# Moving matmul operands by 8 to 48 bytes off multiples of 64 in SBUF, in a two-layer trunk on one core

## The reference

```python
def short_conv_mixer(h, w_in, conv_w, w_out):
    bcx = h @ w_in                       # 1024 -> 3 x 1024
    u = c_gate * xp
    u_conv = causal_depthwise_conv3(u)
    return (b_gate * u_conv) @ w_out

def swiglu(h, w_gate, w_up, w_down):
    return (jax.nn.silu(h @ w_gate) * (h @ w_up)) @ w_down

for i in range(2):
    mixer = mla_mixer if i == 0 else short_conv_mixer
    h = h + mixer(rms_norm(h))
    h = h + swiglu(rms_norm(h))
return rms_norm(h)
```

## Time and profile before

| | |
|---|---|
| median of 3 runs | 1104.34 us (1103.94 to 1104.73) |
| the profiled execution's own time | 1105.14 us |
| its span in the trace | 1103.4 us, so 1.7 us lie around it |
| TensorE busy | 98% |
| LDWEIGHTS busy | 87% |
| VectorE busy | 67% |
| ScalarE busy | 41% |
| DMA | 26.7% of 16 engines, 96 GB/s |
| TensorE on the chain that ended last | 93% |

### The profile page before, as it was taken

The page is one execution under the profiler, slowest core; times in us unless marked ns, Lnnn a source line. Parts: engine busy times, 40 slices in busy tenths (PEclk is TensorE's granted clock), DMA queues, the critical chain, the costliest instruction groups (busy, mean ns, idle before and its releaser), DMA issues.

```text
span 1103.4 us, 16219 instructions
## 1 busy us (share of the span) xinstructions
PE 1081.8 (98%) x6208; PEld 956.0 (87%) x6208; DVE 734.9 (67%) x1013; ACT 454.2 (41%) x621; POOL 40.7 (4%) x22
## 2 busy tenths in 40 slices
PE   9999999998999999999999999999989999999997
PEld 7888888887999999888888888888879999988886
DVE  6667766698788887733447446677878888773332
ACT  5667763333445545521231212224345455452221
POOL 0232230000000000000000000000000000000000
PEclk9999999999899999999999999999989999999999
DMA  7211211322232232232222332223222332222211
GB/s 272 102 67 48 76 50 65 115 87 95 87 114 89 101 114 105 77 105 105 105 76 77 115 115 85 107 76 115 77 83 108 114 114 79 112 105 105 72 61 76
DMA packets 16964, 106.17 MB, mean 96 GB/s; under 512 B 1889, under 2 KB 2145, under 8 KB 6433
## 3 DMA queue, kind: packets, MB, share of 16 engines
q1 hardware_dynamic: 16848, 105.43, 26.7%
q0 software_dynamic: 80, 0.26, 0.1%
HBM read 103.59 MB, written 2.10 MB: 96 GB/s over the span
## 4 chain that ended last, share of the span: by engine, by line
PE 93%; DVE 4%; ACT 1%; DMA 1%; issue 0%; SPq 0%; DVEq 0%; ACTq 0%
PE bank L453 31%; PE bank L454 30%; PE bank L455 30%; PE bank L607 1%; PE bank L593 1%; DMA head<-head_in 1%; DVE w_lo L1450 0%; DVE x_lo L1481 0%; ACT w_hi L1007 0%; DVE rstd L1178 0%; DVE s_lo L1452 0%; DVE work L1183 0%; ACT w_hi L793 0%; DVE work L1442 0%; DVE work L1440 0%
## 5 line engine op out<-in xcount | busy, mean ns | idle before, releaser
L793 ACT ACTIVATE w_hi<-raw 128x2048 fp32r<-128x2048 f32 (+1 forms) x66 | 118.6, 1797 | 277.9 <-PE bank L455 277.8
L1146 DVE TENSOR_TENSOR w_lo<-raw,w_hi 128x2048 fp32r<-128x2048 f32 (+2 forms) x58 | 126.8, 2186 | 104.1 <-ACT w_hi L793 104.1
L453 PE MATMUL bank<-x_hi,w_hi 128*128 128x256 f32 x512 | 146.3, 286 | 10.5 <-DVE inner L1508 10.5
L454 PE MATMUL bank<-x_lo,w_hi 128*128 128x256 f32 x512 | 146.0, 285 | 0.0
L455 PE MATMUL bank<-x_hi,w_lo 128*128 128x256 f32 x512 | 145.9, 285 | 0.0
L453 PE MATMUL bank<-inner_hi,w_hi 128*128 128x512 f32 x352 | 137.0, 389 | 0.0
L454 PE MATMUL bank<-inner_lo,w_hi 128*128 128x512 f32 x352 | 137.0, 389 | 0.0
L455 PE MATMUL bank<-inner_hi,w_lo 128*128 128x512 f32 x352 | 136.9, 389 | 0.0
L453 PE MATMUL bank<-a_hi,w_hi 128*128 128x512 f32 x296 | 117.2, 396 | 1.9 <-DVE a_lo L1236 1.5
L455 PE MATMUL bank<-a_hi,w_lo 128*128 128x512 f32 x296 | 115.4, 390 | 0.0
L454 PE MATMUL bank<-a_lo,w_hi 128*128 128x512 f32 x296 | 115.3, 390 | 0.0
(11 more groups left out here) (207 smaller groups left out, 2111.3 us busy)
## 6 DMA issues: line engine op xcount, KB each, us to landing
raw<-weights_in SPq DMA_DIRECT2D x82, 1024.0 KB, 4.8
raw<-weights_in SPq DMA_DIRECT2D x12, 768.0 KB, 4.2
raw<-weights_in SPq DMA_DIRECT2D x6, 512.0 KB, 3.7
work<-x SPq DMA_DIRECT2D x4, 512.0 KB, 6.1
head<-head_in SPq DMA_DIRECT2D x3, 512.0 KB, 8.5
out<-head SPq DMA_DIRECT2D x3, 512.0 KB, 3.3
out<-head SPq DMA_DIRECT2D x2, 256.0 KB, 4.0
head<-head_in SPq DMA_DIRECT2D x1, 293.5 KB, 3.5
```

Of the source, the lines that this page charges most:

```text
L453: pe.matmul(o, lhs[0], rhs[0], start=start, stop=False, skip_group_check=True)
L454: pe.matmul(o, lhs[0], rhs[1], start=False, stop=False, skip_group_check=True)
L793: act.activation(w_hi[s][:, 0:n], raw[s][:, 0:n], ACT.Copy).then_inc(hi_split[s], 1)
L1146: v.tensor_tensor(w_lo[s][:, 0:n], raw[s][:, 0:n], w_hi[s][:, 0:n], ALU.subtract).then_inc(w_split[s], 1)
```

## The change

Only places in SBUF change. Each tensor that TensorE reads gets a start that is moved by some bytes; `placed` learns to place at any multiple of 4 bytes (it allocates from the multiple of 32 below and slices). Four 8-column tensors of the softmax move into the arena, since the row is nearly full.

```diff
+LINE = 64
+SLOT_OFF = (4, 2)
-SUMS_AT = [0, 6 * TILE_BYTES]
-FORMS_AT = 12 * TILE_BYTES
-INNER_AT = 40 * TILE_BYTES
+SUMS_AT = [16, 6 * TILE_BYTES + 48]
+FORMS_AT = 12 * TILE_BYTES + LINE + 0
+INNER_AT = 40 * TILE_BYTES + 2 * LINE
 INNER_HI_AT = 0
-FFN_IN_AT = INNER_AT + 2 * PLAIN_ROUNDS * TILE_BYTES
-MIXER_IN_AT = KF * TILE_BYTES
-CONV_AT = HEAD_OUT_AT = (0, KD * TILE_BYTES)
+FFN_IN_AT = INNER_AT + 2 * PLAIN_ROUNDS * TILE_BYTES + 0
+MIXER_IN_AT = KF * TILE_BYTES + LINE + 32
+HEAD_OUT_AT = (0, KD * TILE_BYTES)
+CONV_AT = (16, KD * TILE_BYTES + 16)
+NUMBERS_AT = 18 * TILE_BYTES
-MID_AT = [(38 + i * MID_TILES) * TILE_BYTES for i in range(2)]
+MID_AT = [(38 + i * MID_TILES) * TILE_BYTES + 2 * LINE for i in range(2)]
...
-            return nc.alloc_sbuf_tensor_at(name, [P, cols], dt, offset=arena_at + at)
+            off = at % 32
+            return nc.alloc_sbuf_tensor_at(name, [P, cols + off // 4], dt, offset=arena_at + at - off)[:, off // 4:off // 4 + cols]
...
-        w_hi = [sb(f"w_hi{s}", SLOT, F32R) for s in range(2)]
-        w_lo = [sb(f"w_lo{s}", SLOT, F32R) for s in range(2)]
+        w_hi, w_lo = ([sb(f"{n}{s}", SLOT + LINE // 4, F32R)[:, off:off + SLOT] for s, off in enumerate(SLOT_OFF)] for n in ("w_hi", "w_lo"))
...
-        row_max, exp_bias, row_sum, row_inv = (sb(n, 8) for n in ("row_max", "exp_bias", "row_sum", "row_inv"))
+        row_max, exp_bias, row_sum, row_inv = (placed(n, NUMBERS_AT + 32 * i, 8, F32)
```

More of the change, by code:

```diff
@@ L89 @@
 TILE_BYTES = SEQ * 4
-SUMS_AT = [0, 6 * TILE_BYTES]
-FORMS_AT = 12 * TILE_BYTES
-INNER_AT = 40 * TILE_BYTES
-INNER_HI_AT = 0
-FFN_IN_AT = INNER_AT + 2 * PLAIN_ROUNDS * TILE_BYTES
-MIXER_IN_AT = KF * TILE_BYTES
-CONV_AT = HEAD_OUT_AT = (0, KD * TILE_BYTES)
+LINE = 64
[3 more added lines that the diff above has]
+INNER_AT = 40 * TILE_BYTES + 2 * LINE
+INNER_HI_AT = 0
+FFN_IN_AT = INNER_AT + 2 * PLAIN_ROUNDS * TILE_BYTES + 0
[3 more added lines that the diff above has]
+NUMBERS_AT = 18 * TILE_BYTES
 SIN_AT, SQ_AT = 16 * TILE_BYTES, 17 * TILE_BYTES
-MID_AT = [(38 + i * MID_TILES) * TILE_BYTES for i in range(2)]
-ARENA = (38 + 2 * MID_TILES) * TILE_BYTES
+MID_AT = [(38 + i * MID_TILES) * TILE_BYTES + 2 * LINE for i in range(2)]
+ARENA = (38 + 2 * MID_TILES) * TILE_BYTES + 2 * LINE
 PI_BELOW = 3.1415925
@@ L205, in build @@
         ident, ones = sb("ident", P), sb("ones", P)
-        row_max, exp_bias, row_sum, row_inv = (sb(n, 8) for n in ("row_max", "exp_bias", "row_sum", "row_inv"))
+        row_max, exp_bias, row_sum, row_inv = (placed(n, NUMBERS_AT + 32 * i, 8, F32)
+                                               for i, n in enumerate(("row_max", "exp_bias", "row_sum", "row_inv")))
         numbers = sb("numbers", 9 * TOK + 2)
```

## The result

The changed kernel takes 1111.59 us (median of 3 runs, 1110.77 to 1112.41) against 1104.34 us: a ratio of 1.0062, 95% interval 1.0048 to 1.0077 (the ratios here are those on record, which differ a little from the quotient of the two medians). It is slower by 7.25 us, where 11.9 us less were forecast. The profiled execution took 1110.77 us, 5.6 us more than that of before, and its span is 1109.0 us.

The account below looks back on a forecast made before the run. TensorE's start-to-start rate, with about 13 ns extra per matmul, was taken as the bound; 8.9 us (256 columns) plus 3.0 (512) made 11.9 us, so 1105.1 - 11.9, less 0.8, gave 1092.4 us, range 1062 to 1116.

Parts of the forecast that it names:

- What bounds the kernel: TensorE, busy 98% of the span: its start-to-start rate, with about 13 ns per matmul belonging to no column, none at half clock.
- That position matters: All TensorE matmuls: the extra depends on how the weight and moving streams stand to one another, so moved starts change it.
- at 512 columns ... I take 1 ns less: All 2952 matmuls of 512 columns: 1 ns less each, 3.0 us, with nearest rows on both sides (220 and 230).
- special case: Before, all stream pairs start on the same byte of every 512; spread positions would likelier move the mean towards lower rows.
- The step at 256 columns: All 2688 matmuls of 256 columns: 117 ns as in the attention rows, 3.3 ns less each, 8.9 us.
- Slower: the streams no longer settle: 512-column matmuls stay at 230 to 232 ns: 13 us more, 1117 us if 256 columns stay at 120; chance 0.22.
- the prediction's upper bound: Every 512-column matmul at 232 ns, 15.6 us more, plus 7.2 us for `a` and `u` touching another line: together 23 us.
- Much more of the extra goes: All 5640 matmuls lose half of the 13.3 ns or more: 38 us, 1067 us; chance 0.20 (below 1078).
- What costs nothing: VectorE and ScalarE on moved tensors keep their durations, a faster TensorE still finds its inputs, DMA targets stay on multiples of 64.

Follow-up runs that it names:

- matmuls-only kernels: Kernels without the computation, running only matmuls at 512 and 256 columns with operand starts varied; at distance 0 the scan in steps of 64 read 226.7 and 120.0 ns.
- scan in steps of 8: Matmuls alone, stationary operand 0 to 248 bytes past the moving one in steps of 8; lowest 226.7 ns at 512 columns, 113.3 at 256.
- scans with steps of 64 and of 8: Matmuls alone, operand starts shifted mainly in steps of 64 bytes, or the stationary one in steps of 8; both read 226.7 and 120.0 ns at distance 0.
- the kernel with the forms moved by 192: Against the kernel before: Winograd forms (moving operand, 256 columns) start 192 bytes further, weights 256 bytes on; 1092.07 us, ratio 0.9879.
- Two whole kernels with the same distances: Against the kernel before: weights 128, 192, 256 and 320 bytes on, 1115.77 us; the same steps with every TensorE operand also 16 bytes on, 1109.90 us.

## Why the prediction was wrong

- **What bounds the kernel.** Right: TensorE's time from start to start, 13.3 ns above its columns, none at half clock, and the same whatever the other engines do. The matmuls-only kernels show the same 226.7 and 120.0 with nothing beside them.
- **That position matters.** Right, and now shown: nothing but places changed in any of the whole kernels. The Trainium skill ("SBUF — State Buffer", SBUF: two separate sides, and "TensorE: Matmul & The Clock Gate", Step-by-step) has two independent read ports for the two streams; the runs do not show which part of the chip makes them meet, but they show that moving one operand alone changes the time from start to start, from 226.7 to 233.3 ns, which a reader of that rule would not expect.
- **The step that failed** is "at 512 columns ... I take 1 ns less", with its reason that before is a special case and new positions spread over many relations, so that the mean would move towards the lower rows. It is a special case, but at 512 columns none is better. The scan in steps of 8 has none of 32 distances below 226.7 and most of them 3 to 7 ns above. Measured: 10.3 us more over the stages of 512 columns in the table (4.1 ns on each of their 2502 matmuls), instead of 3.0 less on 2952.
- **The step at 256 columns** had the right sign and was too large: 5.4 us won instead of 8.9, 2.0 ns on each of 2688. There the place of before is among the slowest of the scan in steps of 8: 26 of the 32 distances read below its 120.0 and none above, so that the same argument held at this width. The size of 3.3 ns came from three starts in attention, where the operands stand as everywhere before the change; that it came near was luck.
- **What was overlooked** stood in the table of starts that I had drawn up with the change: the allocation gives the four weight tensors steps of 64 between them (144, 200, 272 and 328 bytes). I treated the start within 64 bytes as what counts. The kernel with those steps alone lost 10.7 us, that with the bytes alone 9.9.
- **The rivals.** "Slower: the streams no longer settle" was the one that came, and 1111.59 us lies where the prediction had put most of its chance, with three relations following each other in each product and a mean at 512 columns of 231 ns. Its price of 13 us was for 256 columns unchanged; its measure is 10.3 less the 5.4 won. "They no longer settle" is not quite so: they settle, on other sequences. The six starts of 232 ns after the change of width at 441.88 in the earlier trace rows went into the prediction's upper bound only. In the scans with steps of 64 and of 8, too, the starts at the head of every case are slower than its settled rate, by 1 to 4 ns in most, and at 512 columns no case settles below 226.7. That was the row to weigh more. The line of that rival on attention, that its rows "show 231 as often in attention as 227", is not in the earlier trace rows: they show a mean of 230 and one of 220.
- **"Much more of the extra goes"** held only at 256 columns and at few placements: 6.7 ns less at a distance of 64, in the kernel with the forms moved by 192. The 2.5 ns of extra that the Trainium skill gives for an isolated matmul ("TensorE: Matmul & The Clock Gate", Back-to-back issue gap) was reached in no case: the smallest are 6.7 ns at 256 columns and 13.3 at 512.
- **What costs nothing.** Right for VectorE (1753 against 1752 ns for `s_lo`) and ScalarE (1485 against 1484 for `s_hi`), for TensorE's inputs in the Winograd rounds, where its waits did not grow, and for DMA (a chunk lands after 4.8 us in both).

The stages explain 5.0 of the 5.6 us between the profiled executions; the medians differ by 7.25 us, of which the part beyond is not traced. Some of it may be the median of before: in the later rounds that kernel took 1105.1 to 1105.3 us, against which the difference is 6.3 to 6.5. Why the rate repeats every 256 bytes stays open, as does what chooses between two sequences of one placement.

## What to carry to other kernels

Where TensorE starts a matmul and a load of weights side by side without waits, read the time from start to start, not the busy time, and compare it with the columns alone. If it has an extra that other engines don't touch, scan the distance of the two operands' starts over 256 bytes in a kernel of matmuls alone, for each width in use, before placing anything, and check the rate again in the whole kernel, since one placement can have two rates: here 0 is right for 512 columns and 64 for 256, and moving only the 256-column operand gained 1.2% where moving all of them lost 0.6%. Keep tensors that share a role at the same place within 256 bytes: room added to each of them moves every later one by a further step.

## What was not expected of the hardware

- In steps of 64 the rate depends on the distance between the two operands with a period of 256 bytes: 226.7, 233.3, 232.1 and 228.9 ns at 512 columns, 120.0, 113.3, 118.6 and 117.8 at 256, for 0, 64, 128 and 192 bytes.
- It is not the distance alone: both operands 16 bytes past a multiple of 64 read 230.0 or 233.4 ns, both on a multiple 226.7. Two whole kernels with the same distances, 16 bytes apart in place, take 1115.77 and 1109.90 us.
- The rate is mostly a short sequence that repeats (229, 231, 229, 231, or 235, 232, 235, 232), and one placement can hold more than one: 228.9 and 233.3 ns for the same case in one execution, 226.7 and 233.3 for a distance of 16 in two scans.
